# A hybrid retention and attention block: who stores the last feed-forward units, how the down product is added up, and where three weight roundings stand

## The chip, the cores and the metric

The kernel runs on one core of a Trainium2 chip. The metric is the device time of one execution in microseconds (us), the median over repeated runs. A core has five instruction queues that work side by side and meet only at semaphores: TensorE (PE), VectorE (DVE), ScalarE (ACT), GpSimd (POOL) and SyncE (SP, which here only issues DMAs). ACT can issue DMAs too.

## The reference, cut to what matters

One layer over 1024 tokens of width 1024, in float32. A mixer (retention and forgetting attention) gives the residual rows `x`; it is over before the change begins. What follows is the channel sub-layer and a last norm:

```
h2  = modulate(rms_norm(x, norm2_w), sh2, sc2)
ffn = (silu(h2 @ w_gate) * (h2 @ w_up)) @ w_down      # D_FF = 2816
x   = x + g2 * ffn
out = rms_norm(x, norm_f_w)
```

## The kernel before, in words

**Split numbers.** Each float32 operand of a product is kept as a high part (`hi`, rounded to the type that TensorE takes, written by ACT with a Copy) and a low part (`lo`, value minus `hi`, written by POOL or DVE with one subtraction). Each product is three matmuls (`passes`, lines 1237 to 1239): hi*hi, hi*lo, lo*hi.

**Seven products for eight.** Gate and up, and later down, are taken as 2x2 block products with seven block products ("units", `Q7 = 7`) in place of eight (Strassen-Winograd). That costs extra additions: sums of weight blocks on POOL, sums of inputs and of results on DVE.

**Gate and up stage.** For p = 0 to 21 (`FT = 22` slices of D_FF, 128 wide) TensorE does seven units of 12 matmuls. Per p, ACT rounds seven weight blocks (`weight_hi(n)`, n = 7p + u, into a ring of 10 buffers), POOL forms the four sums and seven low parts (`gate_up_units`), ACT copies three PSUM banks into `snap` (`snapshot`) and takes two Silus, DVE adds (`combine`). For p of 1 and more, TensorE's unit 2 waits for snapshot 0 of p and unit 4 for snapshot 2 of p, since the bank is written again. Before p = 1, ACT has rounded the seven input blocks of p = 0 (`unit_hi`, in the order 0, 3, 1, 5, 4, 2, 6), done its first copies and Silus, and only then come `weight_hi(10)` to `weight_hi(14)` (line 1723).

**The f units.** Two slices p make one pair m (0 to 10). From them DVE forms three sums and one more (`f_sum`), ACT rounds seven blocks (`f_hi(m, l)`), DVE writes their low parts (`f_lo(m, l)`, counted by `x_lo`), and SP stores each hi/lo unit of 512 KB in the DRAM tensor `f_units` (`unit_store`, line 523). Unit e = 7m + l uses buffer e mod 3, so `f_hi` of unit e waits (`x_out`) until unit e - 3 is stored. There are 77 units. SP's list stores e = 65 to 76 after p = 20, interleaved with loads for the down stage.

**Down stage.** Three chunks of the 11 pairs (3, 4 and 4), each with seven products l = 0 to 6 of four PSUM banks b; a bank takes 9 matmuls in chunk 0 and 12 in the others. For chunk c, product l is g = 7c + l. `down_units` loads `da` from `f_units`; `down_raw` loads blocks of `w_down` (`db11`, `db21`, `db12`, `db22`). POOL multiplies them by g2 (`scale`), forms sums (`T1`, `T2`, ...) and the low parts of l = 0, 2, 4, 6 (`low`); ACT rounds (`down_hi(g)`, after product g - 3 has ended); DVE writes the low parts of l = 1, 3, 5 (`down_lo`). All of POOL's operations are 1536 elements wide in chunk 0 and 2048 in the others. On POOL the order in a chunk is: scale 0, scale 1, low 0, scale 2, T1, low 2, scale 3, T2, the `db12` sum, low 4, the `db21` sum, low 6.

**Adding up.** ACT copies the banks of l = 0 to `dn1`. DVE evacuates the others: l = 1 is added into `res2` (the residual rows, loaded from `mid_rows` after the last f unit is stored), l = 2 gives `dn3`, l = 3 gives `dn2`, l = 4, 5 and 6 are added into `res2`. The blocks `dn1`, `dn3` and `dn2` are added into `res2` right after l = 1, 2 and 3, each with one DVE instruction of 128x2048 (lines 2437 to 2450). TensorE waits with bank b of l = 3 until bank b of l = 1 is evacuated; with l = 4 until that of l = 3; with l = 6 until that of l = 4; with l = 0 of the next chunk until that of l = 5 (line 1325 and around it, semaphore `d_ev`).

**The end.** With l = 5 and 6 of chunk 2 the rows are normed (`norm_steps`, `last_rows`) and stored.

Of the kernel before, what the change touches and what calls it, by code (L numbers as in the profile page):

```python
# [10 lines left out]
ALU = mybir.AluOpType  # L11
# [7 lines left out]
HALF = 512  # L19
# [21 lines left out]
Q7 = 7  # L41
# [32 lines left out]
def hybrid_block(nc, x, c, ada_w, ada_b, norm1_w, w_in, b_f, ret_proj, fox_proj, w_out, norm2_w,  # L74
# [19 lines left out]
    with ctx:  # L94
# [220 lines left out]
        d_raw = [sem(f"d_raw{i}") for i in range(4)]  # L315
        d_res = sem("d_res")

# [86 lines left out]
        def _(sp):  # L404
# [170 lines left out]
            down_raw(0, 3)  # L575
            down_units(0, 0)
            unit_store(FT // 2 - 2, 2)
            unit_store(FT // 2 - 2, 3)
            down_units(0, 1)
            unit_store(FT // 2 - 2, 4)  # L580
            down_units(0, 2)
            unit_store(FT // 2 - 2, 5)
            unit_store(FT // 2 - 2, 6)
            for l in range(Q7):
                unit_store(FT // 2 - 1, l)
            sp.wait_ge(c_comb, comb(FT - 1, 5))
# [4 lines left out]
            for i in range(2):  # L591
                sp.dma_start(res2[:, 4 * i:4 * i + 4], mid_rows[4 * i:4 * i + 4].rearrange("t p d -> p t d")).then_inc(d_res, 16)
            for ch in range(len(CHUNKS)):
# [20 lines left out]
        def _(pool):  # L614
# [136 lines left out]
            for c in range(len(CHUNKS)):  # L751
# [24 lines left out]
                pool.wait_ge(d_sum, AFTER_STATE + 4 * c + 1)  # L776
                low(2, T1)
                scale(3, db22, 1)
# [3 lines left out]
                else:  # L782
                    pool.wait_ge(u_used, AFTER_QK + Q7 * FT)
                pool.tensor_tensor(T2, db22[:, 0:n_m], T1, ALU.subtract).then_inc(d_sum, 1)  # L784
                pool.tensor_tensor(db12[:, 0:n_m], db22[:, 0:n_m], db12[:, 0:n_m], ALU.subtract).then_inc(d_sum, 1)
                pool.wait_ge(d_sum, AFTER_STATE + 4 * c + 3)
# [547 lines left out]
        def _(act):  # L1334
# [342 lines left out]
            for u in (1, 5, 4, 2, 6):  # L1677
                unit_hi(u)

            def silu(i, at, p):  # L1680
# [3 lines left out]
            def f_hi(m, l):  # L1684

                if m < 0:
                    return
                e = Q7 * m + l
                x, y = fb[:, 2 * m % 3], fb[:, (2 * m + 1) % 3]
                if l in (0, 1, 6):  # L1690
                    act.wait_ge(c_comb, comb(2 * m + 1, 5))
                else:
                    act.wait_ge(x_sum, AFTER_ST + 4 * m + l - 1)
                src = (x[:, 0], y[:, 0], fsum[:, 0], fsum[:, 1], x[:, 1], y[:, 0], y[:, 1])[l]
                if e >= 3:
                    act.wait_ge(x_out[e % 3], 16 * (e // 3))
                act.activation(fu[:, e % 3, 0, :], src, ACT.Copy).then_inc(x_hi, 1)


# [22 lines left out]
            silu(1, 6, 0)  # L1722
            for n in range(10, 15):
                weight_hi(n)
            for p in range(1, FT):
# [15 lines left out]
                if odd:  # L1741
                    f_hi(m, 3)
                snapshot(1, Y, 1)
                weight_hi(n + 2)
                if odd:
                    f_hi(m, 4)
                snapshot(2, X, 2)
                weight_hi(n + 3)
                f_hi(m, 5 if odd else 0)
                silu(0, comb(p, 1), p)  # L1750
                weight_hi(n + 4)
                if p == FT - 1:
# [4 lines left out]
                if p == FT - 1:  # L1757
                    down_hi(1)
                weight_hi(n + 6)
# [3 lines left out]
            for l in range(Q7):  # L1763
                f_hi(FT // 2 - 1, l)
            for c in range(len(CHUNKS)):
                for l in range(Q7):
                    g = Q7 * c + l
                    if l == 0:
                        if c > 0:
                            act.wait_ge(d_ev, AFTER_OUT + 24 * (c - 1) + 12)  # L1770
                        else:
                            act.wait_ge(u_used, AFTER_QK + Q7 * FT)
                        for b in range(4):
                            act.wait_ge(d_pj, AFTER_OUT + 4 * g + b + 1)
                            act.activation(dn1[:, b, :], ps[:, bank_of(c, l, b), :], ACT.Copy).then_inc(d_copy, 1)
                    down_hi(g + 2)
# [18 lines left out]
        def _(dve):  # L1795
# [591 lines left out]
            f_sum(m, 2)  # L2387
            f_lo(m, 0)
            down_lo(1)
            f_lo(m, 1)  # L2390
            f_sum(m, 3)
# [5 lines left out]

            def block_of(i, j):
                return res2[:, 4 * i:4 * i + 4, j * HALF:(j + 1) * HALF]

# [8 lines left out]
            for c in range(len(CHUNKS)):  # L2409
                last = c == len(CHUNKS) - 1  # L2410
                for l in range(Q7):
                    g = Q7 * c + l
                    down_lo(g + 2)
                    i, j = ((0, 0), (0, 0), (0, 0), (0, 0), (1, 1), (0, 1), (1, 0))[l]
                    if l == 4:
                        dve.wait_ge(d_add, AFTER_ST + 3 * c + 2)
                    elif l == 5:
                        dve.wait_ge(d_add, AFTER_ST + 3 * c + 3)
                    elif l == 2:
                        dve.wait_ge(d_copy, AFTER_OUT + 4 * c + 4)  # L2420
                    if c == 0 and l == 1:
                        dve.wait_ge(d_res, 32)
                    for b in range(4):
                        if l == 0:
                            break
                        dve.wait_ge(d_pj, AFTER_OUT + 4 * g + b + 1)
                        x = ps[:, bank_of(c, l, b), :]
                        o = res2[:, 4 * i + b, j * HALF:(j + 1) * HALF]
                        if l == 2:
                            tt(dn3[:, b, :], x, dn1[:, b, :], ALU.add).then_inc(d_ev, 1)  # L2430
                        elif l == 3:
                            tt(dn2[:, b, :], x, dn1[:, b, :], ALU.add).then_inc(d_ev, 1)
                        else:
                            tt(o, x, o, ALU.add).then_inc(d_ev, 1)
                        if last and l >= 5:
                            norm_steps(2, b + 4 * (l - 5), last_rows)
                    if l == 1:
                        dve.wait_ge(d_copy, AFTER_OUT + 4 * c + 4)
                        if c > 0:
                            dve.wait_ge(d_ev, AFTER_OUT + 24 * c)  # L2440
                        o = block_of(1, 0)
                        tt(o, o, dn1[:, :, :], ALU.add).then_inc(d_add, 1)
                    elif l == 2:
                        dve.wait_ge(d_ev, AFTER_OUT + 24 * c + 8)
                        o = block_of(1, 1)
                        tt(o, o, dn3[:, :, :], ALU.add).then_inc(d_add, 1)
                    elif l == 3:
                        dve.wait_ge(d_ev, AFTER_OUT + 24 * c + 12)
                        o = block_of(0, 1)
                        tt(o, o, dn2[:, :, :], ALU.add).then_inc(d_add, 1)  # L2450
            for t in range(TT, TT + 3):
# [25 lines left out]
```

## Time and profile before

| | us |
|---|---|
| median of 3 runs (2017.89 to 2021.26) | 2019.42 |
| the profiled execution's own time | 2022.69 |
| its span, from the first to the last instruction | 2020.9 |
| PE busy | 1885.1 (93%) |
| DVE busy | 1087.9 (54%) |
| POOL busy | 1049.7 (52%) |
| ACT busy | 631.6 (31%) |

The mean granted TensorE clock is 0.981 of full speed (2.4 GHz). In time from the span's start: the gate and up stage begins at about 1316 us, p = 1 soon after 1346, the down stage at 1762, and the last matmul ends at about 2010. A timeline row reads: start, duration, engine, line, operation, output and inputs, count; in brackets how long the engine had been idle before it, and what ended that. Rows of one kind that follow closely are merged (x2, x3), and their time then covers all of them with what lies between.

### The profile page before, as it was taken

Reading aid. Unit: us, or ns where it says so; the run is one execution under the profiler, and the core shown is the slowest. Engines: PE = TensorE matmul, PEld = TensorE weight load, DVE = VectorE, ACT = ScalarE, POOL = GpSimd, SP = SyncE. Lnnn points to the kernel's source line nnn. Section 1 sums busy time; section 2 is a strip of 40 time slices with the busy share of each in tenths; the row PEclk is TensorE's granted clock in tenths of the full one; section 3 lists DMA queues with packets and bytes.
Section 4 is the critical chain, followed back from the end, with each engine's and each line's share of the span. In section 5 each row is a group of like instructions: output and inputs, shape, how many; then the busy total and the mean of one; then the engine's idle time right before and its main releaser. Section 6 shows DMA issues by size and latency. Waiting matters only on the chain.

```text
span 2020.9 us, 23796 instructions
## 1 busy us (share of the span) xinstructions
PE 1885.1 (93%) x8788; PEld 1559.6 (77%) x8788; DVE 1087.9 (54%) x1560; ACT 631.6 (31%) x1142; POOL 1049.7 (52%) x577
## 2 busy tenths in 40 slices
PE   2888999999999999999999999969999999879897
PEld 2676888888788888888878888758888888758775
DVE  4875555454545555455555343564565564662636
ACT  4431232414232223332231101454444444321212
POOL 2522525353533333333325657647887887667951
PEclk9998999999999999999999999989999999989999
DMA  9361111111321111111114212313444544687543
GB/s 354 98 226 57 53 33 52 32 49 35 108 71 42 42 42 42 42 42 42 42 61 147 73 47 74 131 31 105 156 153 146 160 147 144 248 336 262 219 183 125
DMA packets 157394, 224.91 MB, mean 111 GB/s; under 512 B 5500, under 2 KB 118012, under 8 KB 153988
## 3 DMA queue, kind: packets, MB, share of 16 engines
q1 hardware_dynamic: 151766, 200.99, 30.5%
q10 hardware_dynamic: 5554, 22.92, 3.1%
q8 instruction: 47, 0.77, 0.2%
q14 instruction: 27, 0.22, 0.0%
HBM read 170.90 MB, written 52.99 MB: 111 GB/s over the span
## 4 chain that ended last, share of the span: by engine, by line
PE 78%; DVE 9%; issue 4%; DMA 3%; ACT 3%; POOL 2%; SPq 0%; DVEq 0%; ACTq 0%; POOLq 0%
PE ps L797 52%; PE ps L1237 8%; PE ps L1239 8%; PE ps L1238 8%; DVE b_res L1800 2%; PE ps L1125 2%; DMA b_ada_ring<-in_ada_w 1%; DMA b_macc<-in_ada_w 1%; DVE b_fu L1800 1%; DVE b_macc L1886 1%; POOL b_wu L717 1%; POOL b_db L758 1%; POOL b_dsum L784 1%; DMA f_units<-b_fu 1%; ACT b_db L1715 1%
## 5 line engine op out<-in xcount | busy, mean ns | idle before, releaser
L797 PE MATMUL ps<-b_hT,b_w_split 128*128 128x512 f32 x3120 | 770.4, 397 | 5.4 <-DVE b_rm L1800 2.0
L797 PEld LDWEIGHTS ps<-b_hT,b_w_split 128*128 128x128 f32 x3120 | 573.4, 189 | 120.3 <-issue 3.4
L632 POOL TENSOR_TENSOR b_spare<-b_w_stage 1x1 f32<-1x1 f32 x89 | 25.3, 284 | 719.6 <-PE ps L797 643.9
L1237 PE MATMUL ps<-b_act_q,b_wu 128*128 128x512 f32 x616 | 241.8, 392 | 17.0 <-DVE b_act_q L1800 8.7
L633 POOL TENSOR_SCALAR b_w_split<-b_w_stage 128x1024 fp32r<-128x1024 f32 x89 | 245.9, 2763 | 0.2 <-issue 0.2
L1238 PE MATMUL ps<-b_act_q,b_wu 128*128 128x512 f32 x616 | 240.9, 391 | 0.0
L1239 PE MATMUL ps<-b_act_q,b_wu 128*128 128x512 f32 x616 | 240.7, 391 | 0.0
L635 POOL TENSOR_TENSOR b_w_split<-b_w_stage,b_w_split 128x1024 fp32r<-128x1024 f32 x89 | 218.7, 2457 | 7.4
L717 POOL TENSOR_TENSOR b_wu<-b_raw,b_wu 128x512 fp32r<-128x512 f32 x110 | 162.1, 1483 | 97.8 <-ACT b_wu L1643 97.3
L1237 PE MATMUL ps<-b_db,b_da 128*128 128x512 f32 x308 | 124.7, 405 | 33.3 <-DVE b_dn L1800 12.6
L1237 PEld LDWEIGHTS ps<-b_act_q,b_wu 128*128 128x128 f32 x616 | 116.4, 189 | 43.7 <-issue 12.2
L1800 DVE TENSOR_TENSOR b_cb<-ps,b_snap 128x512 f32<-128x512 f32 x66 | 45.4, 688 | 177.5 <-PE ps L1239 176.8
L1239 PEld LDWEIGHTS ps<-b_act_q,b_wu 128*128 128x128 f32 x616 | 116.3, 189 | 24.5
L1238 PEld LDWEIGHTS ps<-b_act_q,b_wu 128*128 128x128 f32 x616 | 116.5, 189 | 24.1
L1800 DVE TENSOR_TENSOR b_macc<-ps,b_macc 128x512 f32<-128x512 f32 x176 | 114.6, 687 | 28.9 <-PE ps L797 28.9
L1238 PE MATMUL ps<-b_db,b_da 128*128 128x512 f32 x308 | 123.2, 400 | 0.0
L1239 PE MATMUL ps<-b_db,b_da 128*128 128x512 f32 x308 | 123.2, 400 | 0.0
L1529 ACT ACTIVATE b_probs<-b_probs,b_smax 128x128 f32<-128x128 f32 (+3 forms) x64 | 49.8, 779 | 199.9 <-DVE b_smax L2101 199.9
L1237 PEld LDWEIGHTS ps<-b_db,b_da 128*128 128x128 f32 x308 | 60.2, 195 | 49.0 <-issue 34.7
L1800 DVE TENSOR_TENSOR b_pT<-ps,b_pT 128x512 fp32r<-128x512 f32 (+1 forms) x96 | 53.4, 556 | 82.1 <-ACT b_pT L1545 81.6
L797 PE MATMUL ps<-b_fy,b_w_split 128*128 128x512 f32 x384 | 89.1, 391 | 0.0
L797 PE MATMUL ps<-b_kst,b_w_split 128*128 128x512 f32 x384 | 87.7, 389 | 0.0
(209 smaller groups left out, 2969.2 us busy)
## 6 DMA issues: line engine op xcount, KB each, us to landing
f_units<-b_fu SPq DMA_DIRECT2D x77, 512.0 KB, 2.7
b_w_stage<-in_w_in SPq DMA_DIRECT2D x65, 512.0 KB, 4.1
b_da<-f_units SPq DMA_DIRECT2D x14, 2048.0 KB, 7.8
b_macc<-in_ada_w SPq DMA_DIRECT2D x13, 1024.0 KB, 5.0
b_raw<-in_w_gate SPq DMA_DIRECT2D x22, 512.0 KB, 4.9
b_raw<-in_w_up SPq DMA_DIRECT2D x22, 512.0 KB, 6.1
b_da<-f_units SPq DMA_DIRECT2D x7, 1536.0 KB, 12.8
b_ada_ring<-in_ada_w SPq DMA_DIRECT2D x10, 1024.0 KB, 9.7
```

Of the source, the lines that this page charges most:

```text
L632: pool.tensor_tensor(spare[0:1, :], src[0:1, 0:1], src[0:1, 0:1], ALU.add)
L633: pool.tensor_scalar(hi, src, 1.0, None, ALU.mult).then_inc(w_hi[slot], 1)
L635: pool.tensor_tensor(lo, src, f(hi), ALU.subtract).then_inc(w_ready[slot], 1)
L717: pool.tensor_tensor(wu[:, n % RING, 1, :], src, f(wu[:, n % RING, 0, :]), ALU.subtract).then_inc(u_rdy, 1)
L758: pool.tensor_tensor(o, o, grow2[:, j * HALF:(j + 1) * HALF].unsqueeze(1).to_broadcast([P, n_m, HALF]), ALU.mult).then_inc(d_scale, 1)
L797: return pe.matmul(o, l, r, start=start, stop=stop)
L1125: last = pe.transpose(ps[:, 4 + n % 2, blk(t - 4 * g)], probs[:, at:at + P], ident)
L1237: pe.matmul(o, l[0], r[0], start=begin and at == 0, stop=False, skip_group_check=go_on)
L1238: pe.matmul(o, l[0], r[1], start=False, stop=False, skip_group_check=go_on)
L1239: return pe.matmul(o, l[1], r[0], start=False, stop=at == end, skip_group_check=go_on)
L1529: act.activation(p, p, ACT.Exp, bias=smax[:, 1, t:t + 1], accum_out=smax[:, 2, t:t + 1]).then_inc(a_e, 1)
L1800: return dve.tensor_tensor(o, a, b, op)
```

## The change: what it does

1. **Stores.** Units e = 65 to 76 are stored by ACT (`late_store`) and no longer by SP. Each `late_store(e)` first waits on ACT's queue for the low part of e. In p = 21 one stands before `f_hi(9, 4)` and snapshot 2, one after snapshot 2, one after the first Silu and before `down_hi(0)`, one after the second Silu and before `down_hi(1)`; the others follow one `f_hi` each. SP issues the loads of `da` for g = 0, 1, 2 without stores between them.
2. **DVE.** The three block additions of 128x2048 of a chunk become twelve of 128x512 (`add_part`): two after each evacuation of l = 4, one after each of l = 5. `down_lo(1)` comes one `f_lo` later. The load of `res2` has two semaphores, so that l = 1 waits for the first half alone. ACT's first copy of chunks 1 and 2 also waits for all twelve additions of the chunk before.
3. **POOL.** `low(2)` moves behind scale 3 and T2.
4. **Weight roundings.** `weight_hi(10)`, `(11)` and `(12)` move from behind the first Silus to behind `unit_hi(4)`, `(2)` and `(6)`.

```diff
-            down_units(0, 0)
-            unit_store(FT // 2 - 2, 2)
...
-            for l in range(Q7):
-                unit_store(FT // 2 - 1, l)
+            for g in range(3):
+                down_units(0, g)
...
-                low(2, T1)
                 scale(3, db22, 1)
...
                 pool.tensor_tensor(T2, db22[:, 0:n_m], T1, ALU.subtract).then_inc(d_sum, 1)
+                low(2, T1)
...
             for u in (1, 5, 4, 2, 6):
                 unit_hi(u)
+                if u in (4, 2, 6):
+                    weight_hi({4: 10, 2: 11, 6: 12}[u])
...
+            def late_store(e):
+                act.wait_ge(x_lo, AFTER_TR + e + 1)
+                act.dma_start(f_units[e % Q7, e // Q7], f(fu[:, e % 3]).rearrange("p a c -> p (a c)")).then_inc(x_out[e % 3], 16)
+            LATE = Q7 * (FT // 2 - 2) + 2
...
                 snapshot(1, Y, 1)
+                if p == FT - 1:
+                    late_store(LATE)
                 weight_hi(n + 2)
                 if odd:
                     f_hi(m, 4)
                 snapshot(2, X, 2)
+                if p == FT - 1:
+                    late_store(LATE + 1)
...
                 f_hi(m, 5 if odd else 0)
                 silu(0, comb(p, 1), p)
                 weight_hi(n + 4)
                 if p == FT - 1:
+                    late_store(LATE + 2)
                     down_hi(0)
...
             for l in range(Q7):
                 f_hi(FT // 2 - 1, l)
+                late_store(LATE + 4 + l)
+            late_store(LATE + 4 + Q7)
...
                             act.wait_ge(d_ev, AFTER_OUT + 24 * (c - 1) + 12)
+                            act.wait_ge(d_add, AFTER_ST + 12 * c)
...
+            def add_part(i, b, j, part, evacuated):
+                dve.wait_ge(d_ev, AFTER_OUT + evacuated)
+                o = row_part(i, b, j)
+                tt(o, o, part[:, b, :], ALU.add).then_inc(d_add, 1)
...
+                        if l == 4:
+                            add_part(0, b, 1, dn2, 24 * c + 8 + b + 1)
+                            add_part(1, b, 1, dn3, 24 * c + 12 + b + 1)
+                        elif l == 5:
+                            add_part(1, b, 0, dn1, 24 * c + 16 + b + 1)
...
-                    if l == 1:
-                        dve.wait_ge(d_copy, AFTER_OUT + 4 * c + 4)
-                        if c > 0:
-                            dve.wait_ge(d_ev, AFTER_OUT + 24 * c)
-                        o = block_of(1, 0)
-                        tt(o, o, dn1[:, :, :], ALU.add).then_inc(d_add, 1)
```

## Rows read from the trace of the kernel before

**Rows 1.** The page's first part: busy time, share and count of each engine.

```profile
PE 1885.1 (93%) x8788; PEld 1559.6 (77%) x8788; DVE 1087.9 (54%) x1560; ACT 631.6 (31%) x1142; POOL 1049.7 (52%) x577
```

**Rows 2.** Timeline of PE: matmuls ahead of which it was idle.

```profile
1358.76 0.77 PE L1237 MATMUL ps<-b_act_q,b_wu 128*128 128x512 f32 x1 [7.22 <-POOL b_wu L717]
...
1762.01 0.76 PE L1237 MATMUL ps<-b_db,b_da 128*128 128x512 f32 x1 [5.25 <-issue]
...
1781.71 0.77 PE L1237 MATMUL ps<-b_db,b_da 128*128 128x512 f32 x1 [9.84 <-ACT b_dn L1775]
...
1813.79 0.76 PE L1237 MATMUL ps<-b_db,b_da 128*128 128x512 f32 x1 [3.80 <-DVE b_dn L1800]
...
1876.06 0.47 PE L1237 MATMUL ps<-b_db,b_da 128*128 128x512 f32 x1 [2.13 <-DVE b_res L1800]
...
1891.61 0.76 PE L1237 MATMUL ps<-b_db,b_da 128*128 128x512 f32 x1 [4.39 <-DVE b_dn L1800]
...
1976.30 0.47 PE L1237 MATMUL ps<-b_db,b_da 128*128 128x512 f32 x1 [4.36 <-DVE b_dn L1800]
```

**Rows 3.** Timeline of PE: neighbouring matmuls soon after a wait, and later.

```profile
1763.43 0.63 PE L1237 MATMUL ps<-b_db,b_da 128*128 128x512 f32 x1
1763.85 0.63 PE L1238 MATMUL ps<-b_db,b_da 128*128 128x512 f32 x1
...
1769.21 0.39 PE L1238 MATMUL ps<-b_db,b_da 128*128 128x512 f32 x1
1769.44 0.39 PE L1239 MATMUL ps<-b_db,b_da 128*128 128x512 f32 x1
```

**Rows 4.** Timeline of DVE, end of gate and up, and the down stage.

```profile
1749.34 2.81 DVE L1800 TENSOR_TENSOR b_fu<-b_fsum,b_fu 128x512 fp32r<-128x512 f32 x1
...
1762.39 7.86 DVE L1800 TENSOR_TENSOR b_fu<-b_fb,b_fu 128x512 fp32r<-128x512 f32 x2
...
1818.43 0.68 DVE L1800 TENSOR_TENSOR b_res<-ps,b_res 128x512 f32<-128x512 f32 x1
...
1877.63 4.39 DVE L1800 TENSOR_TENSOR b_res<-b_res,b_dn 128x2048 f32<-128x2048 f32 x1
```

**Rows 5.** Timeline of POOL, start of p = 1, and the down stage.

```profile
1349.42 1.82 POOL L717 TENSOR_TENSOR b_wu<-b_raw,b_wu 128x512 fp32r<-128x512 f32 x1 [24.34 <-ACT b_wu L1643]
...
1744.66 6.95 POOL L758 TENSOR_TENSOR b_db<-b_db,b_grow 128x1536 f32<-128x1536 f32 x2 [8.19 <-DMA b_db<-in_w_down]
...
1761.88 3.92 POOL L758 TENSOR_TENSOR b_db<-b_db,b_grow 128x1536 f32<-128x1536 f32 x1
1765.88 3.82 POOL L775 TENSOR_TENSOR b_dsum<-b_db 128x1536 f32<-128x1536 f32 x1
...
1875.26 4.62 POOL L764 TENSOR_TENSOR b_db<-b_db 128x2048 fp32r<-128x2048 f32 x1 [2.09 <-ACT b_db L1715]
...
1889.38 5.90 POOL L764 TENSOR_TENSOR b_db<-b_db 128x2048 fp32r<-128x2048 f32 x1 [2.87 <-ACT b_db L1715]
1895.24 11.24 POOL L758 TENSOR_TENSOR b_db<-b_db,b_grow 128x2048 f32<-128x2048 f32 x2
```

**Rows 6.** Timeline of ACT: a DMA issue, p = 21, start of down.

```profile
1053.26 0.46 ACTq L1563 DMA_DIRECT2D b_resid<-in_x  x1
...
1745.92 0.60 ACT L1732 ACTIVATE b_snap<-ps 128x512 f32<-128x512 f32 x1 [1.60 <-PE ps L1239]
...
1756.94 1.47 ACT L1715 ACTIVATE b_db<-b_db 128x1536 fp32r<-128x1536 f32 x1
...
1780.99 2.04 ACT L1775 ACTIVATE b_dn<-ps 128x512 f32<-128x512 f32 x4
```

**Rows 7.** SP's timeline at 1784; DMA issues: count, KB each, us to landing.

```profile
1784.55 0.92 SPq L592 DMA_DIRECT2D b_res<-mid_rows  x2
...
b_da<-f_units SPq DMA_DIRECT2D x1, 1536.0 KB, 15.8
...
f_units<-b_fu SPq DMA_DIRECT2D x9, 512.0 KB, 2.7
```

More of the change, by code:

```diff
@@ L315, in hybrid_block @@
         d_raw = [sem(f"d_raw{i}") for i in range(4)]
-        d_res = sem("d_res")
+        d_res = [sem(f"d_res{i}") for i in range(2)]
         u_sum, u_hi, u_rdy, u_used, h_tr, h_mdd, h_mda = r_sw, r_m, r_chain, r_rot, r_hi, r_qk, r_v
@@ L575, in _ @@
             down_raw(0, 3)
-            down_units(0, 0)
-            unit_store(FT // 2 - 2, 2)
[L578 to L583, printed above, removed]
-            for l in range(Q7):
-                unit_store(FT // 2 - 1, l)
+            for g in range(3):
+                down_units(0, g)
             sp.wait_ge(c_comb, comb(FT - 1, 5))
@@ L591, in _ @@
             for i in range(2):
-                sp.dma_start(res2[:, 4 * i:4 * i + 4], mid_rows[4 * i:4 * i + 4].rearrange("t p d -> p t d")).then_inc(d_res, 16)
+                sp.dma_start(res2[:, 4 * i:4 * i + 4], mid_rows[4 * i:4 * i + 4].rearrange("t p d -> p t d")).then_inc(d_res[i], 16)
             for ch in range(len(CHUNKS)):
@@ L1722, in _ @@
             silu(1, 6, 0)
-            for n in range(10, 15):
+            for n in range(13, 15):
                 weight_hi(n)
@@ L1757, in _ @@
                 if p == FT - 1:
+                    late_store(LATE + 3)
                     down_hi(1)
@@ L2388, in _ @@
             f_lo(m, 0)
+            f_lo(m, 1)
             down_lo(1)
-            f_lo(m, 1)
             f_sum(m, 3)
@@ L2396, in _, with row_part @@
             f_lo(m, 6)
-            def block_of(i, j):
-                return res2[:, 4 * i:4 * i + 4, j * HALF:(j + 1) * HALF]
+            def row_part(i, b, j):
+                return res2[:, 4 * i + b, j * HALF:(j + 1) * HALF]
+            def add_part(i, b, j, part, evacuated):
+                dve.wait_ge(d_ev, AFTER_OUT + evacuated)
+                o = row_part(i, b, j)
+                tt(o, o, part[:, b, :], ALU.add).then_inc(d_add, 1)
             def last_rows(t):
@@ L2414, in _ @@
                     i, j = ((0, 0), (0, 0), (0, 0), (0, 0), (1, 1), (0, 1), (1, 0))[l]
[L2415 to L2419, printed above, removed]
+                    if l == 2:
                         dve.wait_ge(d_copy, AFTER_OUT + 4 * c + 4)
-                    if c == 0 and l == 1:
-                        dve.wait_ge(d_res, 32)
+                    if c == 0 and l in (1, 4):
+                        dve.wait_ge(d_res[l // 4], 16)
                     for b in range(4):
@@ L2427, in _ @@
                         x = ps[:, bank_of(c, l, b), :]
-                        o = res2[:, 4 * i + b, j * HALF:(j + 1) * HALF]
+                        o = row_part(i, b, j)
                         if l == 2:
@@ L2433, in _ @@
                         else:
+                            if l >= 5:
+                                dve.wait_ge(d_add, AFTER_ST + 12 * c + (2 * b + 1 if l == 5 else 8 + b + 1))
                             tt(o, x, o, ALU.add).then_inc(d_ev, 1)
+                        if l == 4:
[3 more added lines that the diff above has]
+                            add_part(1, b, 0, dn1, 24 * c + 16 + b + 1)
                         if last and l >= 5:
                             norm_steps(2, b + 4 * (l - 5), last_rows)
-                    if l == 1:
-                        dve.wait_ge(d_copy, AFTER_OUT + 4 * c + 4)
-                        if c > 0:
-                            dve.wait_ge(d_ev, AFTER_OUT + 24 * c)
-                        o = block_of(1, 0)
-                        tt(o, o, dn1[:, :, :], ALU.add).then_inc(d_add, 1)
[L2443 to L2450, printed above, removed]
             for t in range(TT, TT + 3):
```

## The prediction

> **What bounds the kernel now.** I read the page's busy shares first: TensorE is at work for 93% of the span, every other engine for at most 54% [rows 1]. So a part of the change counts only where it moves a wait of TensorE. Its timeline shows seven such waits near the change [rows 2]: 7.22 us in p = 1, 5.25 us before the first down product, 9.84 us before the second, and from then on one before l = 4 of each chunk (3.80, 4.39, 4.36 us) and one before l = 3 of chunks 1 and 2 (2.13 us each, one row stands for both). After such a wait the matmuls start 0.42 us apart, later 0.23 us apart [rows 3]: TensorE is granted the lower of its two levels (1.2 GHz) for about seven matmuls, then 2.4 GHz. That makes each long wait about 1.4 to 1.8 us dearer.
>
> Then I read VectorE beside GpSimd, since the change touches both. An addition with both inputs in SBUF waits for whatever GpSimd is doing: 128x512 took 2.81 us when it started inside GpSimd's pair 1744.66 to 1751.6 and ended 0.6 us behind it; two neighbours took 7.86 us, over two GpSimd instructions that end at 1765.80 and 1769.70 [rows 4, 5]. The second was not served behind the first; GpSimd's next one came between, and took 3.82 us. The block addition at 1877.63 ended 2.1 us after GpSimd's instruction that ends at 1879.88. An addition that reads PSUM isn't held up: 0.68 us at 1818.43, inside a busy GpSimd. So the free prices are 0.6 us (128x512) and 2.1 us (128x2048), a GpSimd instruction is 3.5 us in chunk 0 (half of 6.95) and 4.6 us later [rows 5], and while GpSimd works without a pause each SBUF addition of VectorE costs one whole GpSimd instruction.
>
> **Part 4, weight roundings.** The wait of 7.22 us ends when a chain ACT, GpSimd, ACT is through; GpSimd had stood idle for 24.34 us until `weight_hi(10)` and took up the low part at 1349.42 [rows 5]. With the rounding at 1328 three GpSimd instructions (low 3, a sum, low 4; 1.25 us each) move up among VectorE's additions there, which TensorE waits for, and push them back by 3 x 1.25 = 3.8 us (gate and up of p = 0 ends 3.5 us later). Behind that remain low 5, low 6 and one sum in place of six operations. Following the chain I get snapshot 0 of p = 1 at 1357.2 in place of 1358.6, so 1.5 us gained, and the wait shrinks to about 2.3 us, before which the clock hardly falls (1876.06 starts with 0.47, not 0.76 [rows 2]). Between 0 and -3.8 us, I take **-2.0**. It is half hidden since most of what is gained was VectorE's free road.
>
> **Part 1, stores.** In p = 21 ACT's queue is in order. `late_store(65)` waits for the low part of unit 65, which VectorE writes after the addition of TensorE's unit 3 (ends 1748.6), and that write ended at 1752.15 (1749.34 + 2.81 [rows 4]). Behind it on ACT stands snapshot 2, done at 1745.92 before [rows 6], and TensorE's unit 4 waits for that. With the issue (0.46 us [rows 6]), `f_hi(9, 4)` and the snapshot (0.6 us each) unit 4 starts at 1753.9, not 1748.6: TensorE loses 5.3 us and 1.4 us of clock. The next two stores wait for units 4 and 5 in the same way, and `down_hi(0)` behind them comes at 1762.9 in place of 1756.94. With its 1.47 us and low 0 (3.4 us) the first down product starts at 1767.9 in place of 1762.01, +5.9. Nothing is gained against that: a store costs SP about a third of a us to issue, and the loads that it delayed were in place long before their products.
>
> From there GpSimd has in after: low 0, scale 2, T1, then, by **part 3**, scale 3 and T2 with no wait. VectorE needs five SBUF operations in this run (the last product of slice 21, two low parts, two f sums), each behind one GpSimd instruction; the second f sum ends at 1784.8 in place of 1771.5. The other low parts, roundings and stores take about 1.5 us a unit, as they did. The last `late_store` is then through at 1795.7, and only behind it ACT copies l = 0, for which the second down product waits: 1796.3 in place of 1781.71 [rows 2, 6], +14.6. `res2` is loaded from 1798.4 (1784.55 before), and `da` for g = 3 behind it, 15.8 us to landing [rows 7], so l = 3 starts at 1815.5. It has 8.2 us of matmuls, and l = 4 follows without the old 3.80 us since the block additions are gone from before it: 1823.7 in place of 1813.79. **+9.9** up to l = 4 of chunk 0. Bounds: 0 where the stores find their low parts ready, +20 where their landing (2.7 us [rows 7]) is slowed by the loads beside it.
>
> A rule speaks on this. The Trainium skill, "DMA: Bandwidth & Descriptors", section "Issuing engines are not separate DMA queues": issuing from more engines saves only the sequencer's issue time. By the rule alone part 1 would be worth nothing either way; by the rows the wait in ACT's order costs, which the rule does not weigh.
>
> **Part 2 and 3, the additions.** Call the start of l = 4 of a chunk t0. GpSimd's low 6 starts 2 us behind it (in chunk 1: 1889.38 [rows 5], before t0 only since t0 was late), and then comes the next chunk's preparation without a pause. It was scale 0, scale 1, low 0, scale 2, T1; with part 3 scale 3 and T2 join, eight instructions. In just this stretch stand the eight quarter additions of l = 4. At 4.6 us + 0.6 us a turn: low 6 ends at t0 + 6.6, the first addition at 7.2, the eighth at 7.2 + 7 x 5.2 = 43.6, and l = 5 bank 0 is evacuated behind it at 44.2. The products of l = 4, 5, 6 are 3 x 48 matmuls of 0.227 us = 32.7 us, and l = 0 of the next chunk waits for that evacuation: it starts at t0 + 44.3, 11.6 us late. Then l = 0 to 3 run through, 43.6 us and 1.5 us of clock, as the waits of 2.13 and 4.36 us are gone (low 3 comes earlier, the block additions are not ahead of l = 3). From l = 4 to l = 4: 44.3 + 43.6 + 1.5 = 89.4 us in place of 1976.30 - 1891.61 = 84.7. **+4.7** for chunk 1 to 2.
> For chunk 0 to 1 the products of l = 4 to 6 are 24.5 us, low 6 takes 3.5 us and starts at 1.8: the eighth addition ends at 5.9 + 7 x 5.2 = 42.3, l = 0 starts at 42.9, then 45.4: 88.3 in place of 1891.61 - 1813.79 = 77.8. **+10.5**. In the last chunk GpSimd has only low 6 left, so the quarters go through; two of l = 5 fall into VectorE's closing chain, about **+0.3**. Bounds of these: each quarter at 0.6 us gives 24.5 + 45.4 = 69.9 and 32.7 + 45.1 = 77.8, so -7.9 and -6.9; above, one more GpSimd turn each, +5.
>
> On the port itself the Trainium skill ("SBUF — State Buffer", section "SBUF: two separate sides") says the pair of ports is an exclusive lock, held for a whole instruction by whoever starts first, and that a VectorE operation with two SBUF inputs is concerned. By that rule alone nothing says who is served next, and VectorE might take several quarters in one turn; the 7.86 us row says that they alternate, and I go by the row.
>
> **Sum.** -2.0 + 9.9 + 10.5 + 4.7 + 0.3 = +23.4 us. The profiled execution took 2022.69 us (its span is 2020.9), so its like would take 2046.1. It lay 3.3 us above the median of 2019.42; on that the change gives 2042.8, and I say 2042.
>
> **Rivals.**
> - *The quarters slip in.* If VectorE gets the port for each quarter at 0.6 us (two neighbours in one turn, or GpSimd pausing for a load), the waits before l = 4 and l = 3 go and no new one comes. Sum: -2.0 + 9.9 - 7.9 - 6.9 + 0.3 = -6.6, 2013. For it: scale 1 of the next chunk needs a load that is issued only after low 6, a pause of a us or two. Against it: one pause isn't seven, and the 7.86 us. It decides below some 2.5 us a quarter: then eight quarters and four evacuations fit into l = 4 to 6. Faster. 0.13.
> - *The start is covered.* If the low parts are ready when ACT comes to its stores, only the port costs: +2 in place of +9.9, 2035. Against it: the first store waits for TensorE's own unit 3. 0.17.
> - *The start is worse.* The ring of three buffers turns slower from ACT, as each store stands behind the next rounding and shares the DMA engines with 3 MB of loads: +10 more, 2052. 0.10.
> - *Gains and losses cancel* (half the quarters slip in, the start is covered): within 4 us of 2019. 0.05.
>
> The forecast itself has 0.55, with 2034 to 2050 as its own range. With the start covered and a part of the quarters slipping in the time comes down to some 2023, with a slower start it goes to 2052; that is my range. A measurement of this kernel tells 0.2% (4 us) from no change. Slower by more: 0.55 + 0.17 + 0.10 and a part of the last, 0.83; within: 0.04; faster: 0.13.
>
> **What would show it.** Right: in p = 21 TensorE idle about 5 us before unit 4, and snapshot 2 behind a DMA issue on ACT; the second down product near +14; in l = 4 of chunks 0 and 1 VectorE rows of `res2` from `res2` and `dn`, 128x512, of 4 to 5 us each; TensorE waiting some 11 to 18 us before l = 0 of chunks 1 and 2 for `res2`; no wait before l = 3 or l = 4; a wait of 2 to 3 us in p = 1 in place of 7.22. Wrong: quarters of 0.6 to 1.2 us next to a busy GpSimd, or no wait at the chunks' edges. Then the time is below 2020.

## The result and the profile after

The changed kernel takes 2035.13 us (median of 4 runs, 2032.71 to 2037.61) against 2020.34 us for the kernel before in the same runs (4 runs). The ratio is 1.0081, 95% interval 1.0062 to 1.0100: slower, by 12.5 to 20 us. 2042 us had been forecast, with a range of 2023 to 2052. The profiled execution took 2034.34 us, its span is 2032.4 (2022.69 and 2020.9 before), a difference of 11.5 us in the span.

The timeline of PE after, matmuls ahead of which it was idle. They answer to [rows 2].

```profile
1356.88 0.77 PE L1229 MATMUL ps<-b_act_q,b_wu 128*128 128x512 f32 x1 [2.81 <-POOL b_wu L709]
...
1752.83 0.77 PE L1229 MATMUL ps<-b_act_q,b_wu 128*128 128x512 f32 x1 [5.18 <-ACT b_snap L1733]
...
1768.28 0.47 PE L1229 MATMUL ps<-b_db,b_da 128*128 128x512 f32 x1 [4.22 <-issue]
1795.53 0.76 PE L1229 MATMUL ps<-b_db,b_da 128*128 128x512 f32 x1 [17.21 <-ACT b_dn L1785]
...
1846.01 0.50 PE L1229 MATMUL ps<-b_db,b_da 128*128 128x512 f32 x1 [0.87 <-DVE b_res L1810]
...
1855.97 0.76 PE L1229 MATMUL ps<-b_db,b_da 128*128 128x512 f32 x1 [7.63 <-DVE b_res L1810]
1865.81 0.50 PE L1229 MATMUL ps<-b_db,b_da 128*128 128x512 f32 x1 [1.65 <-DVE b_res L1810]
...
1939.09 0.47 PE L1229 MATMUL ps<-b_db,b_da 128*128 128x512 f32 x1 [2.27 <-DVE b_res L1810]
...
1948.95 0.50 PE L1229 MATMUL ps<-b_db,b_da 128*128 128x512 f32 x1 [1.98 <-DVE b_res L1810]
```

The reader is to see three things. The waits before l = 3 and l = 4 (3.80, 2.13, 4.39, 4.36 us) are gone. In p = 21 there is a new one of 5.18 us, and the one before the second down product has grown from 9.84 to 17.21. At the edge from chunk 0 to chunk 1 there are 0.87 + 7.63 + 1.65 = 10.2 us of waits for `res2`, as the banks in the way were not yet evacuated into it; at the edge to chunk 2 the two long ones are 2.27 + 1.98 = 4.3 us.

ACT after, in p = 21. This is the order that makes the 5.18 us: a DMA issue, the rounding, then the snapshot, which was done at 1745.92 before [rows 6]:

```profile
1742.24 0.60 ACT L1733 ACTIVATE b_snap<-ps 128x512 f32<-128x512 f32 x1 [1.54 <-PE ps L1231]
1751.14 0.33 ACTq L1696 DMA_DIRECT2D f_units<-b_fu  x1
1751.57 0.63 ACT L1691 ACTIVATE b_fu<-b_fb 128x512 fp32r<-128x512 f32 x1 [8.73 <-DVE b_fu L1810]
1752.11 0.58 ACT L1733 ACTIVATE b_snap<-ps 128x512 f32<-128x512 f32 x1
```

VectorE after, from l = 4 of chunk 0 on. Each merged row x2 is a pair of quarter additions (128x512, a quarter of a block):

```profile
1825.46 8.04 DVE L1810 TENSOR_TENSOR b_res<-b_res,b_dn 128x512 f32<-128x512 f32 x2
1833.42 0.68 DVE L1810 TENSOR_TENSOR b_res<-ps,b_res 128x512 f32<-128x512 f32 x1
1834.02 1.28 DVE L1810 TENSOR_TENSOR b_res<-b_res,b_dn 128x512 f32<-128x512 f32 x2
1835.22 0.68 DVE L1810 TENSOR_TENSOR b_res<-ps,b_res 128x512 f32<-128x512 f32 x1
1835.82 9.53 DVE L1810 TENSOR_TENSOR b_res<-b_res,b_dn 128x512 f32<-128x512 f32 x2
1845.27 0.68 DVE L1810 TENSOR_TENSOR b_res<-ps,b_res 128x512 f32<-128x512 f32 x1
1845.87 9.35 DVE L1810 TENSOR_TENSOR b_res<-b_res,b_dn 128x512 f32<-128x512 f32 x2
1855.14 0.68 DVE L1810 TENSOR_TENSOR b_res<-ps,b_res 128x512 f32<-128x512 f32 x1
1855.86 4.31 DVE L1810 TENSOR_TENSOR b_res<-b_res,b_dn 128x512 f32<-128x512 f32 x1
```

And GpSimd beside it:

```profile
1827.89 5.06 POOL L750 TENSOR_TENSOR b_db<-b_db,b_grow 128x2048 f32<-128x2048 f32 x1
1835.15 4.61 POOL L750 TENSOR_TENSOR b_db<-b_db,b_grow 128x2048 f32<-128x2048 f32 x1 [2.21 <-DMA b_db<-in_w_down]
1839.73 5.07 POOL L756 TENSOR_TENSOR b_db<-b_db 128x2048 fp32r<-128x2048 f32 x1
...
1859.69 4.91 POOL L775 TENSOR_TENSOR b_dsum<-b_db,b_dsum 128x2048 f32<-128x2048 f32 x1
```

A pair costs 8 to 9.5 us while GpSimd runs. It costs 1.28 us in the one pause, 2.21 us long, in which GpSimd waits for a block of `w_down`. The row at 1855.14 is the evacuation for which TensorE waits 7.63 us. It reads PSUM, takes 0.68 us, and stands behind 9.35 us of quarters.

The next table shows where the 11.5 us between the two spans lie. Starts of l = 4 after are taken from the end of the product before (ACT's next rounding or VectorE's next evacuation follows it by 0.1 to 0.2 us): 1822.6, 1904.1, 1988.9.

| stretch | before | after | difference | forecast |
|---|---|---|---|---|
| start to first matmul of gate and up | 1316.2 | 1313.9 | -2.4 | 0 |
| to the first addition behind unit 3 of p = 21 | 432.5 | 433.9 | +1.4 | -2.0 |
| to l = 4 of chunk 0 | 65.1 | 74.8 | +9.8 | +9.9 |
| to l = 4 of chunk 1 | 77.8 | 81.5 | +3.7 | +10.5 |
| to l = 4 of chunk 2 | 84.7 | 84.8 | +0.1 | +4.7 |
| to the end | 44.6 | 43.5 | -1.1 | +0.3 |

The first row is not the change's: nothing ahead of it differs between the two kernels. Over all fourteen traces of this case the start of gate and up lies between 1310.4 and 1318.3 us. So times of two traces are compared below as distances from an event ahead of the edit. For the down stage that is the addition behind unit 3 of p = 21, the second row's end: 1748.73 before, 1747.78 after.

### The profile page after: what moved, and what is told of

It reads as the page before. It is cut to its first block, busy times and chain, and to the rows that moved or that the text cites. A ratio compares the mean times of both kernels' runs of the same rounds, so it can differ in the third digit from the quotient of the medians.

```text
span 2032.4 us, 23840 instructions
## 1 busy us (share of the span) xinstructions
PE 1892.4 (93%) x8788; PEld 1564.6 (77%) x8788; DVE 1141.5 (56%) x1587; ACT 631.4 (31%) x1142; POOL 1050.0 (52%) x577
## 4 chain that ended last, share of the span: by engine, by line
PE 79%; DVE 9%; DMA 5%; issue 3%; ACT 2%; POOL 1%; SPq 0%; DVEq 0%; ACTq 0%; POOLq 0%
PE ps L789 51%; PE ps L1229 8%; PE ps L1230 8%; PE ps L1231 8%; DVE b_res L1810 3%; PE ps L1117 2%; DMA b_ada_ring<-in_ada_w 1%; DMA b_macc<-in_ada_w 1%; DMA f_units<-b_fu 1%; DMA b_da<-f_units 1%; DVE b_fu L1810 1%; DVE b_macc L1896 1%; POOL b_wu L709 1%; DVE b_macc L1810 1%; DVE b_hT L1810 1%
## 5 line engine op out<-in xcount | busy, mean ns | idle before, releaser
L1229 PE MATMUL ps<-b_act_q,b_wu 128*128 128x512 f32 x616 | 244.9, 398 | 18.7 <-DVE b_act_q L1810 9.6
L1230 PE MATMUL ps<-b_act_q,b_wu 128*128 128x512 f32 x616 | 244.0, 396 | 0.0
L1231 PE MATMUL ps<-b_act_q,b_wu 128*128 128x512 f32 x616 | 243.9, 396 | 0.0
L1229 PEld LDWEIGHTS ps<-b_act_q,b_wu 128*128 128x128 f32 x616 | 118.2, 192 | 46.4 <-issue 18.4
L1231 PEld LDWEIGHTS ps<-b_act_q,b_wu 128*128 128x128 f32 x616 | 118.3, 192 | 25.3
L1230 PEld LDWEIGHTS ps<-b_act_q,b_wu 128*128 128x128 f32 x616 | 118.3, 192 | 24.3
L1810 DVE TENSOR_TENSOR b_res<-b_res,b_dn 128x512 f32<-128x512 f32 x36 | 88.7, 2489 | 0.4
```

What stands on the lines that cost most here:

```text
L1229: pe.matmul(o, l[0], r[0], start=begin and at == 0, stop=False, skip_group_check=go_on)
L1230: pe.matmul(o, l[0], r[1], start=False, stop=False, skip_group_check=go_on)
L1231: return pe.matmul(o, l[1], r[0], start=False, stop=at == end, skip_group_check=go_on)
L1810: return dve.tensor_tensor(o, a, b, op)
```

## The experiments

Each is timed beside the kernel before on the same chip, and the ratio is to that (medians of the kernel before were 2017.6, 2020.3, 2018.1 and 2020.7 us in the four groups of runs). The first four are the kernel before with one part of the change each; the later place of `down_lo(1)` goes with part 1 in all of them.

### stores_only

```diff
-            unit_store(...)           # SP, units 65 to 76
+            late_store(...)           # ACT, where the change has them
```

> The kernel before with part 1 alone (ACT stores the last twelve units). Theory A, ACT's order holds TensorE up: a wait of about 5 us before unit 4 of p = 21 as in the changed kernel (5.18), the first down product about 6 us later than 1762, the second about 7 us later than 1781.7 (less than the changed kernel's 13.8, since GpSimd stops after T1), and that shift stays to the end: about +7 us, 2027. Rival B, the start of the changed kernel was late because GpSimd's scale 3 and T2 shut VectorE out: the second product within 2 us of before, total +1 to +2.

Measured: 2029.9 us, ratio 1.0065 (1.0047 to 1.0083), +13 us. Its PE timeline:

```profile
1752.91 0.77 PE L1229 MATMUL ps<-b_act_q,b_wu 128*128 128x512 f32 x1 [5.10 <-ACT b_snap L1731]
1767.65 0.77 PE L1229 MATMUL ps<-b_db,b_da 128*128 128x512 f32 x1 [4.22 <-issue]
1789.03 0.77 PE L1229 MATMUL ps<-b_db,b_da 128*128 128x512 f32 x1 [11.38 <-ACT b_dn L1782]
...
1824.34 0.77 PE L1229 MATMUL ps<-b_db,b_da 128*128 128x512 f32 x1 [7.71 <-DVE b_dn L1807]
```

The start came as theory A has it, +5.6 and +7.3 us for the first two products on the two traces' own times, +6.4 and +8.1 us counted from the addition in p = 21. What A missed is the last row: the wait before l = 4 of chunk 0 grows from 3.80 to 7.71 us. The evacuations and the first two block additions come 7.3 us later, as the second product does; but then VectorE's low part of l = 5 meets GpSimd's low 6, which started 0.27 us before it, and takes 4.97 us, not 1.75:

```profile
1818.62 4.97 DVE L1807 TENSOR_TENSOR b_db<-b_db 128x1536 fp32r<-128x1536 f32 x1
```

The evacuation for l = 4 stands behind it, and l = 4 starts 11.3 us late. So the price is 13 us, not 7.

### quarters_only

```diff
-                        tt(o, o, dn1[:, :, :], ALU.add)     # 128x2048, after l = 1, 2, 3
+                            add_part(...)                   # 128x512, after each bank of l = 4, 5
```

> The kernel before with part 2 alone (twelve quarter additions behind l = 4 and 5). Theory A, a quarter costs one GpSimd instruction while GpSimd runs: without scale 3 and T2 GpSimd's run behind l = 3 has six instructions, not eight, VectorE is free about 30 us after the start of l = 4, just before TensorE needs the banks of l = 5 (24.5 us in chunk 0, 32.7 in chunk 1): at most 4 us of waiting at the first edge, none at the second, the waits of 3.80, 4.39 and 4.36 us before l = 4 gone, the 2.13 us before l = 3 still there. About -11 us, 2009. Rival B, the quarters alone make the change slow: waits of 6 to 9 us at both edges as in the changed kernel, total between 0 and +5.

Measured: 2016.36 us, ratio 0.9994 (0.9980 to 1.0008): no change, where theory A had forecast 11 us less; the total is rival B's. The waits before l = 4 went and the 2.13 us before l = 3 stayed, as theory A has it. A also holds at the second edge (0.70 us) and fails at the first, where the waits were 0.85 and 7.62 us. Six GpSimd instructions from low 6 to T1 are enough there, since the products of chunk 0 are short. What the quarters gain before l = 4 they give back at the edge.

### low2_late_only

```diff
-                low(2, T1)
                 scale(3, db22, 1)
                 ...
                 pool.tensor_tensor(T2, ...)
+                low(2, T1)
```

> The kernel before with part 3 alone (GpSimd's low 2 behind scale 3 and T2). Theory A: in chunk 0 scale 3 and T2 shut VectorE out of two f sums, so the second down product comes about 7 us later than 1781.7; in chunks 1 and 2 low 3 is ready early, the 2.13 us before l = 3 go, and the chain low 3, block addition, block addition ahead of l = 4 starts about 9 us earlier, so most of 4.39 and 4.36 goes too. +7 - 13 = about -6 us, 2014. Rival B, it does nothing at the start (second product within 2 us): -13, 2007.

Measured: 2002.26 us, ratio 0.9928 (0.9911 to 0.9944): **faster**, by 11 to 18 us, more than either theory had. Its PE timeline in the down stage:

```profile
1786.47 0.76 PE L1237 MATMUL ps<-b_db,b_da 128*128 128x512 f32 x1 [15.82 <-ACT b_dn L1775]
...
1806.55 0.50 PE L1237 MATMUL ps<-b_db,b_da 128*128 128x512 f32 x1 [1.11 <-DMA b_da<-f_units]
...
1815.61 0.47 PE L1237 MATMUL ps<-b_db,b_da 128*128 128x512 f32 x1 [0.61 <-DVE b_dn L1800]
...
1884.90 0.47 PE L1237 MATMUL ps<-b_db,b_da 128*128 128x512 f32 x1 [0.73 <-DVE b_dn L1800]
```

The second product is 6.3 us late, counted from the addition in p = 21 (39.3 us behind it, 33.0 before), as two f sums waited for scale 3 and T2: 3.96 and 3.79 us in place of 0.68 and 0.69. So theory A is right on the start. But l = 4 now waits 0.61 and 0.73 us in place of 3.80 and 4.39, with the block additions where they were. In chunk 1 VectorE starts low 3 at 1859.45, where it was 1870.58 before, and the chain behind it on VectorE moves with it.

### roundings_only

```diff
             for u in (1, 5, 4, 2, 6):
                 unit_hi(u)
+                if u in (4, 2, 6):
+                    weight_hi({4: 10, 2: 11, 6: 12}[u])
...
-            for n in range(10, 15):
+            for n in range(13, 15):
                 weight_hi(n)
```

> The kernel before with part 4 alone. From the first matmul of gate and up to the first matmul behind the wait in p = 1 the kernel before takes 42.54 us and the changed one 43.02. Theory A, what GpSimd does earlier it takes from VectorE at the same place: this kernel takes 43 us too, total within 1 us of before. Rival B, my prediction of -2 us is right and the changed kernel lost it elsewhere: 40.5 us.

Measured: 2016.15 us, ratio 0.9999 (0.9980 to 1.0018). From first matmul to the one behind the wait: 1353.96 - 1310.93 = 43.0 us, theory A's number. The wait shrank to 2.81 us, but it starts later. ACT's timeline shows one reason: `weight_hi(12)` waits 8.72 us until TensorE's unit 2 of p = 0 sets its buffer of the ring free, and the first snapshot stands behind it. The first two rows are from before, the others from this kernel:

```profile
1342.09 0.60 ACT L1719 ACTIVATE b_snap<-ps 128x512 f32<-128x512 f32 x1 [5.75 <-DVE b_act_q L1800]
...
1348.19 0.63 ACT L1682 ACTIVATE b_cb<-b_cb 128x512 f32<-128x512 f32 x1 [3.07 <-DVE b_cb L1800]
```

```profile
1343.09 0.63 ACT L1643 ACTIVATE b_wu<-b_raw 128x512 fp32r<-128x512 f32 x1 [8.72 <-PE ps L1239]
1343.63 0.58 ACT L1721 ACTIVATE b_snap<-ps 128x512 f32<-128x512 f32 x1
...
1348.41 0.64 ACT L1684 ACTIVATE b_cb<-b_cb 128x512 f32<-128x512 f32 x1 [1.77 <-DVE b_cb L1802]
```

The last row of each is the second Silu of p = 0, behind which the other roundings come. From the first matmul it is 32.0 us before and 37.5 us here, 5.5 us later: 3.3 us since the fifth unit starts later (24.8 us behind the first matmul in place of 21.4), some 1.5 us since eight of its matmuls run at the lower clock (about 0.2 us each), and the rest since the snapshot comes late. What is left behind the Silu takes 5.5 us in place of 10.6.

Then the clock. The same 60 us from the first matmul on, before and in this kernel (columns: busy time and count of PE, PEld, DVE, ACT, POOL, then the granted clock, DMA share, GB/s):

```profile
1316.00:1376.00 60.00, 46.20 (x193) 36.86 (x194) 35.68 (x35) 29.20 (x42) 30.67 (x22) 0.91 0.14 37
```

```profile
1311.00:1371.00 60.00, 49.95 (x187) 39.37 (x187) 36.04 (x33) 28.68 (x41) 30.82 (x21) 0.83 0.11 30
```

The granted clock is 0.83 in place of 0.91, and there are six matmuls fewer in the same time. But that is not what the change fixes. Six traces have part 4. Behind the wait of 2.8 us, 13 matmuls start 0.43 us apart in three of them (changed kernel, this one, whole_blocks_moved), 8 in one (all_but_quarters) and none in two (all_but_stores, snapshot_first), where the granted clock over these 60 us is 0.89. Five of the six had the same waits before, within 0.1 us. From the first matmul to the addition in p = 21 the first three take 433.6 to 434.6 us and the other three 431.4 to 431.7; the eight traces without part 4 take 431.2 to 432.7.

### all_but_quarters, all_but_stores

The changed kernel with part 2, or part 1, undone.

> The changed kernel with its part 2 undone (three block additions of 128x2048 behind l = 1, 2, 3, as before). Part 3 alone gave 2002, part 1 alone +12, part 4 nothing. Theory A, with part 3 in place the quarters cost what they cost at the chunks' edges (waits of 7.63 and 2.27 us and their slow clock): without them TensorE waits less than 1 us at the edges and the sum is 2002 + 12 = about 2014, 20 us below the changed kernel. Rival B, the stores and part 3 add up at the start (VectorE shut out and ACT's order), and the quarters cost little: 2025 or more.

Measured: 2010.85 us, ratio 0.9955 (0.9935 to 0.9975). Theory A: no wait at an edge, and one of 2.12 us before l = 4 of chunk 0. So with part 3 in place the quarters cost 1.0081 - 0.9955 = 1.3%, some 25 us, where alone they cost nothing. From the first matmul of that l = 4 to the last of all this kernel has no wait over 0.5 us and takes 176.7 us; the changed kernel takes 198.6, with 16 us of waits and some 30 matmuls at the lower clock.

> The changed kernel with its part 1 undone (SP stores the last units as before). Theory A: no wait before unit 4 of p = 21; second down product at about 1786.5 as with part 3 alone, not 1795.5; edges as in the changed kernel (waits of about 7.6 us). 9 to 12 us below the changed kernel, 2023 to 2026, so still slower than before. Rival B, the stores are the whole loss: 2005 or less.

Measured: 2026.62 us, ratio 1.0028 (1.0007 to 1.0050), theory A. The second product came at 1784.78, which is 39.3 us behind the addition in p = 21, as with part 3 alone. The first edge's waits were 0.93, 7.62 and 1.97 us. The stores cost 0.5%, about 11 us.

### snapshot_first

```diff
                 snapshot(1, Y, 1)
-                if p == FT - 1:
-                    late_store(LATE)
...
                 snapshot(2, X, 2)
                 if p == FT - 1:
+                    late_store(LATE)
                     late_store(LATE + 1)
```

> The changed kernel with late_store(65) moved from ahead of snapshot 2 of p = 21 to behind it, nothing else. Theory A, the 5.18 us before unit 4 are ACT's order: the wait goes, the first down product comes 3 to 6 us earlier than 1768.3, the second 3 to 6 us earlier than 1795.5, total about 2030. Rival B, the wait is the low part itself and moves to another place: unit 4 on time but the second product within 1 us of 1795.5, total 2035.

Measured: 2028.75 us, ratio 1.0046 (1.0031 to 1.0060), 7 us less than the changed kernel. Unit 4 has no wait any more, and both products come 3.9 us earlier, counted from the addition in p = 21 (4.6 us on the traces' own times):

```profile
1763.66 0.77 PE L1229 MATMUL ps<-b_db,b_da 128*128 128x512 f32 x1 [8.55 <-issue]
1790.92 0.76 PE L1229 MATMUL ps<-b_db,b_da 128*128 128x512 f32 x1 [17.03 <-ACT b_dn L1784]
```

The wait was one of order on ACT. Part of it comes back before the first product (8.55 us in place of 4.22). The 17 us stay: they are ACT's chain of f units. Part 3 alone brings that wait to 15.82 us and the stores alone to 11.38, from 9.84. Of the 7 us of the total, some may be the clock behind part 4's wait, which stayed high in this trace.

### whole_blocks_moved

```diff
-                            add_part(...)                    # 12 x 128x512
+                    if l == 4:
+                        tt(o, o, dn2[:, :, :], ALU.add)      # 3 x 128x2048, same place
+                        tt(o, o, dn3[:, :, :], ALU.add)
+                    if l == (4 if last else 5):
+                        tt(o, o, dn1[:, :, :], ALU.add)
```

> The changed kernel with the same additions behind l = 4 and 5, but as three of 128x2048 per chunk in place of twelve of 128x512. Theory A, each addition with both inputs in SBUF waits for one GpSimd instruction whatever its length: three waits per chunk in place of about eight, VectorE is through with both blocks of l = 4 some 14 us after l = 4 ends, ahead of TensorE's need, no wait at the edges over 1 us; about 20 us below the changed kernel, 2010 to 2014, level with all_but_quarters. Rival B, it is the place (behind l = 4, in GpSimd's busy stretch) and not the number of pieces: waits at the edges of 4 us and more, 2025.

Measured: 2014.61 us, ratio 0.9984 (0.9969 to 0.9998), 20 us below the changed kernel. It is the number of pieces far more than the place: the place leaves 0.3% to all_but_quarters (0.9955), and the intervals of the two touch. The split of the load of `res2` is undone with it, as in all_but_quarters. VectorE at the first edge:

```profile
1834.18 5.23 DVE L1810 TENSOR_TENSOR b_res<-b_res,b_dn 128x2048 f32<-128x2048 f32 x2
...
1842.22 3.82 DVE L1810 TENSOR_TENSOR b_res<-b_res,b_dn 128x2048 f32<-128x2048 f32 x1
```

Two blocks of 128x2048 are through in 5.23 us, where the same additions in eight quarters, with three evacuations between, took 29.8 us (1825.46 to 1855.22). The 5.23 us have luck in them: both blocks met GpSimd's pause, here 2.57 us long. Beside a GpSimd without a pause my estimate for them is 2 x (4.6 + 2.1) = 13.4 us, which no run shows. Theory A asked for no edge wait over 1 us, and the edge has only one of 0.85 us. One of 3.16 us comes later, before l = 2 of chunk 1. It ends with GpSimd's low 2:

```profile
1871.13 4.54 POOL L756 TENSOR_TENSOR b_db<-b_dsum,b_db 128x2048 fp32r<-128x2048 f32 x1
```

GpSimd was held up in its turn: three of its instructions beside VectorE's operations of 128x2048 took 6.26, 6.64 and 6.67 us in place of 4.6, and part 3 had put low 2 behind two more instructions.

### Versions that beat both

```diff
                 if p == FT - 1:
+                    silu(0, comb(p, 1), p)
+                    down_hi(0)
+                    silu(1, comb(p, 3), p)
+                    down_hi(1)
+                    f_hi(m, 5)
+                    f_hi(m, 6)
+                    continue
...
```

This, with part 3 and nothing else of the change, is part3_free_act.

> The kernel before with part 3, and in p = 21 the two Silus, down_hi(0) and down_hi(1) moved ahead of f_hi(9, 5) and f_hi(9, 6), which wait for a buffer. Stores on SP. Part 3 alone waits 5.2 us before the first down product since ACT stands at f_hi(9, 5). Theory A: low 0 comes at about 1751, the wait shrinks to under 1 us, VectorE's and ACT's chain of f units ends about 5 us earlier, and so do the load of res2, l = 3 and the end: 1996 to 1998. Rival B, the stores' landing beside the loads sets when the f units end: the first wait goes but the second grows by as much, 2002.

Measured: 1998.21 us, ratio 0.9899 (0.9868 to 0.9930). The first wait of down is 0.61 us. The second is 16.78, but its product comes 33.9 us behind the addition in p = 21, 5.4 us earlier than with part 3 alone (39.3). GpSimd is through with T2 at 1765.3, so that the two f sums take 0.68 and 0.69 us again. Theory A, and the best version of the study.

> part3_free_act once more, as the version that beats both kernels, with more rounds. Theory: the same 0.99 of the time before (1996 to 2000). Rival: its first ratio (0.9899, interval 0.9868 to 0.993) was drawn low and it is level with part 3 alone (0.993).

Measured: 1998.39 us, ratio 0.9898 (0.9877 to 0.9918). It stands: 21 us below the kernel before, 37 below the changed one. Against part 3 alone (0.9911 to 0.9944) the gain of 0.3% is at the edge of what the intervals tell; that both its traces have the second product at 33.9 us speaks for it.

> part3_free_act (1998.2) with its three block additions moved, whole, behind l = 4 and 5. Theory A: it has only 1.3 us of waits for dn left, and VectorE has the time either way: within 2 us of 1998. Rival B, the move costs at the edges: 2003 or more.

Measured: 2003.32 us, ratio 0.9931 (0.9908 to 0.9953). Rival B rather than A, though the intervals touch: with part 3 the blocks need no other place, and behind l = 4 they bring waits of 0.88 us before l = 0 and 3.13 us before l = 2 of chunk 1, the latter again for GpSimd's low 2.

> part3_free_act with the start of down reordered: ACT copies l = 0 and rounds g = 2 between the roundings of units 71 and 72, SP loads da for g = 3 ahead of the stores of units 72 to 76, res2 has a semaphore for each half and l = 1 waits for the first alone. Theory A, what sets the start of l = 3 is the chain last f unit, store, load of res2, evacuation of l = 1: the wait of 16.8 us before the second product shrinks to under 3 us, and l = 3 starts 6 to 8 us earlier, 1990 to 1992. Rival B, the copies and the rounding between the f units push the last store back by as much: 1997 to 1999.

Measured: 2003.11 us, ratio 0.9930 (0.9912 to 0.9948). Neither theory: the 16.8 us became 9.62 and 6.95 us, and l = 3 starts 52.4 us behind the addition in p = 21, 1.3 us earlier than in part3_free_act. With the rounding of g = 2 moved ahead, GpSimd's low 2 and `db12` sum moved ahead too (1769.41 and 1773.27), into the f units: an f sum of VectorE took 3.84 us in place of 0.69, the next two low parts 4.59 in place of 1.29. The store behind them came at 1777.80, and one rounding waited 6.88 us for it.

## Why the prediction was right, and where it was off

**The sum.** The direction, the two causes and the range held. The size did not: +23.4 us was forecast for the span and +11.5 measured, +22.6 and +14.8 in medians. Nearly all of the gap lies at the two edges between chunks, in part 2. That 2035 is also the number of the rival "The start is covered" is chance, since the start was not covered.

**Part 1, +9.9 up to l = 4 of chunk 0: right**, 9.8 measured, and by the steps named. Unit 4 was to start 5.3 us late, it was 5.18; the first and second products were to come at 1767.9 and 1796.3, they came at 1768.3 and 1795.5. That these agree so closely is in part luck, since this execution was 0.95 us earlier at the addition in p = 21: counted from there they are +7.2 and +14.8 against +5.9 and +14.6. The third step, l = 3 behind the load of `da`, was to come at 1815.5 and came at 1814.3. snapshot_first shows the order on ACT as the cause of the first. That the stores, not part 3, carry most of it is shown by stores_only beside low2_late_only: alone they bring l = 4 of chunk 0 by 11.3 and 3.3 us later. The f sums behind scale 3 and T2 do cost 6.3 us at the second product, but part 3 takes the wait before l = 4 away.

**Part 2, one GpSimd instruction a quarter: the mechanism right, the term mis-sized.** Quarters took 4.0 to 4.8 us each against 5.2 assumed, and the evacuation that TensorE needs stood behind them, as forecast. But I let GpSimd run "without a pause", and that is the step that failed. In its run lies one of 2.2 us at scale 1, in both chunks, for a block of `w_down` whose load is issued only after low 6. The forecast had named it only in a rival, as "a pause of a us or two". In that pause two quarters and an evacuation slip in at 0.6 us, so six of eight quarters wait, not eight, and the first evacuation of l = 5 starts at t0 + 32.5 in chunk 0, not 42.3, and at t0 + 34.2 in chunk 1, not 43.6. The edges then cost 3.7 and 0.1 us and not 10.5 and 4.7. In the trace of before the pause does not show: a block addition held scale 0 up by 2.1 us, just as long as the load was missing (11.24 us for two instructions of 4.6 [rows 5]).

**Part 4, -2.0: wrong.** Two steps failed. The first is the time by which p = 0 is pushed back: 3.5 to 3.8 us was forecast for VectorE's additions alone, and the second Silu came 5.5 us later, by the clock and by ACT's order as well (roundings_only). So the wait did shrink as forecast (2.81 us for 2.3), but the matmul behind it came 43.0 us after the first one, where 41.0 had been forecast and 42.5 was the time before. That `weight_hi(12)` would wait 8.72 us on ACT, ahead of the snapshot, is a wait in an engine's order, of the kind that the forecast had priced in part 1 and not here. The second is the clock, "before which the clock hardly falls": in three of six traces it was at the lower level for 13 matmuls, more than the 5 to 7 behind the old 7.22 us, and in two it did not fall at all. Nor was the 0.47 us of a first matmul a sign of that: at 1976.30 before it is 0.47 too, and seven matmuls behind it start 0.43 us apart. The stretch to p = 21 took 1.4 us more in the changed kernel's trace and 2.0 more in roundings_only, but 0.8 to 1.1 less in the three traces in which fewer matmuls ran slow. The whole time of roundings_only is level with before within 0.2%.

**Part 3** had no term of its own; it was booked with part 2, as what takes the waits of 2.13 and 4.36 us away. The reading under it was not right: beside part 3 the quarters have next to nothing left to gain (2.12 us before one l = 4 in all_but_quarters). Part 3 alone removes nearly all of them and makes the kernel 0.7% faster. Quarters alone remove the waits before l = 4 too, but not those before l = 3. Parts 2 and 3 aim at the same waits, so their gains don't add, while their costs do: part 3 puts two more GpSimd instructions into the stretch in which the quarters stand.

**The rivals.** "The quarters slip in" is refuted by the 8 to 9.5 us a pair, apart from the one pause. "The start is covered" and "the start is worse" are refuted by the stretch of +9.8. "Gains and losses cancel" is refuted by the time itself, 0.6 to 1.0% above before.

Open: why the closing stretch was 1.1 us shorter. No run separates it from differences of a few us that come without any change, as at the start of gate and up. Open too is what sets the clock behind the wait in p = 1: the waits ahead of it do not.

## What to carry to other kernels

- Here an addition of VectorE with both inputs in SBUF waited for about one GpSimd instruction, however short it was: 4.0 to 4.8 us for a 128x512 addition of 0.6 us beside GpSimd instructions of 4.6 to 5.1 us. Beside a busy GpSimd use few long ones and keep what TensorE waits for ahead of them. The long ones hold GpSimd up in turn (6.3 to 6.7 us in place of 4.6).
- Compare two traces from an event just ahead of the edit. On their own times part3_free_act gained 9 us at the second product; counted that way it gained 5.4.
- Before a DMA issue, or a rounding, moves to another place in an engine's queue, write down what stands behind its wait there. Here it was each time a copy for which others waited.
- When several edits aim at the same waits, time each alone: here one part was worth -0.7%, and the others turned it into +0.8%.

## What the runs showed of the hardware that was not expected

- TensorE's granted clock followed neither the last wait nor the waits before it. In five traces with the same waits within 0.1 us (3.3, 1.25, 2.65, then 2.8 us), 13 matmuls behind the last one started 0.43 us apart in three, and none in two. After 7.22 us of waiting 5 to 7 did, in all eight traces without part 4. The difference is worth 2 to 3 us of a stretch of 432.
- Two block additions of 128x2048 went through in 5.23 us in GpSimd's pause for a load, where turns with a busy GpSimd would make it about 13 by my estimate. The second block was still at work when GpSimd's scale 1 started at 1837.63, and scale 1 then took 6.26 us in place of 4.6.
